# Order within a tile's period of block two's attention: scaling one tile ahead, high part in front of the next exponents, low part behind the next maxima

## The reference

```python
s_own = jnp.einsum("bhqd,bhkd->bhqk", qc, ko) * scale          # plus a bias by distance
p = jax.nn.softmax(logits, axis=-1)                            # attention over own tokens
...
s = jnp.einsum("bshd,bmhd->bhsm", q4, mk) * (MEM_DH ** -0.5)
p = jax.nn.softmax(s, axis=-1)                                 # attention over the memory
...
merged = sigmoid(ga + bg[0]) * y_a + sigmoid(gb + bg[1]) * y_b + sigmoid(gc + bg[2]) * y_c
x = x + rmsnorm(merged @ w_out, g_post_mix)
```

## Time and profile before

| what | value |
|---|---|
| median of 3 runs | 1616.34 us (1607.52 to 1617.88) |
| the profiled execution | 1616.58 us, span 1614.8 us |
| PE busy | 1515.2 us, 94% of the span |
| PEld, ACT, POOL, DVE busy | 1256.3, 656.9, 715.7, 583.3 us |
| self part of the attention, first transpose to last PV | 816.1 to 924.6 us |
| mem part | 1002.4 to about 1085 us |

### The profile page before, as it was taken

How to read it: one execution, slowest core, us unless ns; L and a number is a source line. 1 busy time by engine, 2 the same in 40 slices (tenths; PEclk the granted TensorE clock), 3 DMA queues, 4 the chain that set the end, 5 groups by cost and what they waited for, 6 DMA issues and landing times.

```text
span 1614.8 us, 19870 instructions
## 1 busy us (share of the span) xinstructions
PE 1515.2 (94%) x7716; PEld 1256.3 (78%) x7716; DVE 583.3 (36%) x888; ACT 656.9 (41%) x969; POOL 715.7 (44%) x608
## 2 busy tenths in 40 slices
PE   8899978899999999999987989999898999999996
PEld 5799757688888888888955678888787888887885
DVE  5755342523333110413034420433325556554002
ACT  3532453544444332322245443543335444554221
POOL 1466003545455544554412245445434455546452
PEclk9999888899999999999999999999999999999999
DMA  8654025322222222224111223122220222222221
GB/s 353 235 235 144 28 70 110 85 83 100 104 94 81 91 88 91 102 79 157 67 38 53 76 86 126 66 78 92 104 70 35 104 103 79 104 97 79 101 81 60
DMA packets 28491, 162.73 MB, mean 101 GB/s; under 512 B 4584, under 2 KB 4840, under 8 KB 13704
## 3 DMA queue, kind: packets, MB, share of 16 engines
q1 hardware_dynamic: 24960, 151.05, 26.0%
q10 hardware_dynamic: 3464, 10.74, 2.6%
HBM read 157.04 MB, written 4.74 MB: 100 GB/s over the span
## 4 chain that ended last, share of the span: by engine, by line
PE 68%; issue 11%; POOL 9%; DVE 5%; ACT 4%; DMA 3%; POOLq 0%; SPq 0%; ACTq 0%; DVEq 0%
PE ps L1695 60%; POOL WL L778 7%; PE ps L1661 1%; DMA raw<-w_up_dram 1%; DMA adap<-w_ada_dram 1%; POOL WL L742 1%; PE ps L1923 1%; DVE ps L1304 1%; ACT S L1110 1%; PE ps L1904 1%; PE ps L1828 1%; DVE S L1576 1%; PE ps L1617 1%; DVE xT L1309 1%; DVE md L1579 1%
## 5 line engine op out<-in xcount | busy, mean ns | idle before, releaser
L742 POOL TENSOR_TENSOR WL<-raw,WH 128x512 fp32r<-128x512 f32 (+2 forms) x344 | 370.4, 1105 | 541.1 <-ACT WH L858 540.9
L1695 PE MATMUL ps<-hH,WH 128*128 128x512 f32 x1136 | 455.5, 401 | 23.6 <-POOL hL L756 8.8
L1695 PE MATMUL ps<-hL,WH 128*128 128x512 f32 x1136 | 448.8, 395 | 0.0
L1695 PE MATMUL ps<-hH,WL 128*128 128x512 f32 x1136 | 448.0, 394 | 0.0
L778 POOL TENSOR_TENSOR WL<-raw,WH 128x512 fp32r<-128x512 f32 x176 | 246.6, 1432 | 240.4 <-ACT WH L1018 240.4
L1695 PEld LDWEIGHTS ps<-hH,WH 128*128 128x128 f32 x1136 | 216.9, 191 | 74.7 <-issue 26.3
L1695 PEld LDWEIGHTS ps<-hH,WL 128*128 128x128 f32 x1136 | 217.2, 191 | 46.3
L1695 PEld LDWEIGHTS ps<-hL,WH 128*128 128x128 f32 x1136 | 217.1, 191 | 43.8
L858 ACT ACTIVATE WH<-raw 128x1024 fp32r<-128x1024 f32 (+3 forms) x172 | 147.9, 885 | 235.8 <-PE ps L1695 228.2
L1695 PE MATMUL ps<-hidH,WH 128*128 128x512 f32 x352 | 137.9, 392 | 1.1 <-POOL WL L778 1.1
L1695 PE MATMUL ps<-hidL,WH 128*128 128x512 f32 x352 | 136.9, 389 | 0.0
(11 more groups left out here) (279 smaller groups left out, 2181.1 us busy)
## 6 DMA issues: line engine op xcount, KB each, us to landing
raw<-w_up_dram SPq DMA_DIRECT2D x44, 1024.0 KB, 4.8
raw<-w_in_dram SPq DMA_DIRECT2D x36, 1024.0 KB, 4.7
adaw<-w_ada_dram SPq DMA_DIRECT2D x22, 1024.0 KB, 6.5
raw<-w_down_dram SPq DMA_DIRECT2D x16, 768.0 KB, 3.9
raw<-w_down_dram SPq DMA_DIRECT2D x16, 640.0 KB, 3.7
xT<-x_dram ACTq DMA_DIRECT2D x2, 2048.0 KB, 10.0
raw<-w_mem_kv_dram SPq DMA_DIRECT2D x4, 1024.0 KB, 4.6
raw<-w_out_dram SPq DMA_DIRECT2D x4, 1024.0 KB, 4.5
```

The source lines that it names most:

```text
L742: pool.tensor_tensor(WL[:, d % 2, ks, cols], raw[:, d % 2, ks, cols], WH[:, d % 2, ks, cols].bitcast(F32), ALU.subtract).then_inc(lo_done, 1)
L1695: mm = pe.matmul(out, lhs[x], rhs[y], start=(first and i == 0), stop=(last and i == 2))
```

## The change

The handler of DVE's scaling is now a step of its own (`scale2`), which stands one tile ahead, in front of the next tile's maxima. ACT's high part is a step of its own (`hi2`), in front of the next exponents on ACT. The low part `lo2(n)` stands behind the maxima of tile n+2 on DVE and in front of the scaling of tile n+2. The new steps and `lo2` have no share of the pieces any more, so the pieces are dealt to `mid2`, `front2` and `back2` only, and stand at other places between PE's steps. Both the self and the mem part are ordered so. No instruction is added or removed, and the streams of POOL and SP are the same.

```diff
         def attend(first, last, pieces):
-            tiles = [("front2", first), ("front2", first + 1)]
+            tiles = [("front2", first), ("front2", first + 1), ("scale2", first)]
             for n in range(first, last):
                 tiles += [("mid2", n)]
-                if n > first:
-                    tiles += [("lo2", n - 1)]
+                if n + 1 < last:
+                    tiles += [("scale2", n + 1)]
+                tiles += [("hi2", n)]
                 if n + 2 < last:
                     tiles += [("front2", n + 2)]
-                tiles += [("back2", n)]
-            tiles += [("lo2", last - 1)]
-            share = [TILES23[tile[1]][3] + 1 for tile in tiles]
+                tiles += [("back2", n), ("lo2", n)]
+            share = [TILES23[tile[1]][3] + 1 if tile[0] in ("front2", "mid2", "back2") else 0 for tile in tiles]
...
-            def back2(n):
+            def hi2(n):
                 kind, i, c, _, _ = tile2(n)
                 sc.wait_ge(pv2_done, heads_before(n + 1))
...
-            def mid2(n):
+            def scale2(n):
                 kind, _, _, nb, heads = tile2(n)
                 ve.wait_ge(exp2_done, heads_before(n + 1))
```

More of the change, by code:

```diff
@@ L1153, in _ @@
                   "bias_fetch": bias_fetch, "bias_rows": bias_rows, "evac_in2": evac_in2, "bias_load": bias_load, "evac_br": evac_br,
-                  "front2": front2, "mid2": mid2, "back2": back2, "mem_load": mem_load,
+                  "front2": front2, "mid2": mid2, "hi2": hi2, "mem_load": mem_load,
                   "evac_kv": evac_kv, "merge": merge})
@@ L1607, in _ @@
                   "attn_out": attn_out, "up": up,
-                  "bias_rows": bias_rows, "evac_in2": evac_in2, "evac_br": evac_br, "front2": front2, "mid2": mid2,
+                  "bias_rows": bias_rows, "evac_in2": evac_in2, "evac_br": evac_br, "front2": front2, "scale2": scale2,
                   "lo2": lo2, "merge": merge})
```

## The result

The changed kernel takes 1600.44 us (median of 8, 1593.02 to 1606.60), the kernel before 1615.12 us (median of 8, 1607.52 to 1619.80). The ratio is 0.9914, with an interval of 0.9894 to 0.9934, so 10.7 to 17.1 us, 13.9 in the middle. The forecast was 7 us of gain and a range that ended at 1602: the direction was right, the size was half of what came.

The account below looks back on a forecast made before the run. PE bounds the kernel, so only its waits can be won: 14.9 us of old self-part waits against 7.5 new gives 7.4 gain, mem part none; 1616.58 - 7.4 = 1609.2, predicted 1609 us, own range 1606 to 1613, wider range 1602 to 1617.

Parts of the forecast that it names:

- Tiles 2, 4 and 5: Self part, transposes following a PV with no piece behind it: PE waits for the low part, 0.45 + 0.35 + 0.35 = 1.15 us.
- Gate 64: Sigmoid gate of unit 64 on ACT, self part near tile 6: its queue makes PE wait 1.4 us; before, 1.95.
- Gates 65 and 67: Gates of units 65 and 67 on DVE, self part, now in front of the low part: 0.7 us of wait each.
- Gate 68: Gate of unit 68 on ACT, tile 14: queue of exponents, split, gate, PT makes PE wait 3.5 us, the worst.
- Old ones: PE's standing time in the self part before the change, 14.9 us, all counted as going away.
- the bound of 16.4 us: Most the change could win: PE's standing time in self and mem parts, 14.9 + 1.5 us, 1.0% of 1616.6.
- both dips: Two stretches of PE at 1.2 GHz at the self part's start, both taken to stay; the second's going would gain about 1.6 us.
- up to 1.4 goes: Mem part: PE's waits for the scaling, up to 1.4 us, could go; none counted, as the first tile's chain holds part.
- the rival in which all waits are covered: Self part: ACT's queues slip less, only 2.5 us of new waits remain; gain 12.4 to 14, 1602.5 to 1604 us; chance 0.15.
- Waits moved to ACT: Slower rival: ACT's exponents, split, gate and PT queue starts late, 23 us of new waits against 14.9; 1625 us; chance 0.08.
- No gain at the end: Rival: time won in the part is given back behind it or by stretched scalings; 1615 to 1617 us; chance 0.15.
- The table rule: About 1380 ns drain per table switch: gates 64 and 68 each cost 1.38 us more, gain 4.6 instead of 7.4; not adopted.

Follow-up runs that it names:

- the last kernel: Changed kernel with the gates of units 64, 65, 67 and 68 moved behind transposes or low parts, and a piece after every self-part PV: 1593.28 us, ratio 0.9878.

## Why the prediction was wrong

**Right: each new wait.** The forecast had 7.5 us of new waits in the self part at named places; 7.1 came at the same places. Tiles 2, 4 and 5, with no piece behind the PV before, 0.56 + 0.45 + 0.45 for a forecast 1.15. Gate 64 at tile 6, 1.20 for 1.4. Gates 65 and 67 on DVE, at tiles 7 and 12, 0.44 and 0.54 for 0.7 each. Gate 68, 3.50 for 3.5. Gate 66 nothing. That the sum is so near is partly luck: 0.3 us too little at the tiles and 0.6 too much at gates 64, 65 and 67 go against each other. These readings came from laying two queues side by side, instruction by instruction, and the move of gate 68 shows that the queue is the cause. The scaling waits went to zero, but for the very first transposes'.

**Wrong: idle time as the price of a wait.** The step was "New waits: 1.15 + 1.4 + 1.4 + 3.5 = 7.5 us. Old ones: 14.9. Gain 7.4 us in the self part." PE's idle fell by 7.7 (14.9 to 7.2), but the stretch fell by 9.4, and again by 9.5 in the run with the self part alone. PE's busy time fell too, by 1.7 us (94.94 to 93.22 in the windows of the table), for the same instructions. The clock doesn't explain it, since it cost 0.9 us more than before; less the clock's cost (3.1 and 4.0), the busy time fell from 91.8 to 89.2, by 2.6. A reason that fits: the ends of matmuls are modelled. In the changed kernel eight transposes in a row are followed by the next matmul 0.79 us after their start (893.00 to 893.79), 0.10 for each, yet one alone is counted as 0.27 long (the middle value of L1923 in the rows above). At a wait the last matmul's counted end isn't overlapped by the next, so 0.17 us more than the idle is lost; from 19 waits before to 7 after, behind the first transposes, that makes 12 x 0.17 = 2.0 us. And a short wait doesn't show at all. These are the eight transposes of tile 13 before:

```profile
904.58 1.28 PE L1923 MATMUL ps<-ident_t,S 128*128 128x128 f32 x8
904.79 0.29 DVE L1598 TENSOR_TENSOR bufBL<-ps,bufBH 128x128 fp32r<-128x128 f32 x1 [0.76 <-ACT bufBH L1128]
...
905.62 0.48 PE L1695 MATMUL ps<-hH,WH 128*128 128x512 f32 x1
```

No idle is counted, but they take 1.04 us instead of 0.79, since the second four may start only behind the low part, which ended at 905.08. Tile 14 is the same (913.78 to 914.82), so 0.5 us are hidden in the two, and 2.0 + 0.5 is close to 2.6. The other kernels agree roughly: less the clock's cost, PE is busy 91.8 us in the three with 19 or 20 waits, 90.4 with the scaling ahead only (13 waits), 89.1 to 89.5 in the four with 7, and 88.9 in the last one (2). No run changed the waits and nothing else, so this account is argued, not shown. It also corrects the bound of 16.4 us: in the last kernel the self part alone is 17.6 us shorter, more than the 14.9 that PE stood there.

**The clock.** The forecast let both dips stay and priced a further one at 1.6 us without counting it. One more came, behind gate 68, in all three profiles of the new self order. By the estimate of the table the clock cost 0.9 us more there than before, which hides a part of the gain.

**Wrong: the mem part at nothing.** The step was "In the mem part up to 1.4 goes; I count none", for a reason that didn't hold: the wait for the queries lies in front of the first scores and not in the 1.4. It gave 3.1 us alone (2.5 against the kernel without a change) and 3.7 in the changed kernel. The window of the earlier trace rows also ended at 1085.00, and a wait of 0.9 us for PT ended at 1086.47, behind its edge. The idle of 2.3 us and four waits at 0.17 make 3.0; the 0.6 us on top in the changed kernel are within the 0.6 by which this stretch also differs without a change.

With the two measured sizes in the sum the gain is 9.4 + 3.1 = 12.5 us, where the two comparisons gave 13.9 and 12.1. The start was off as well: the sum began at 1616.58, and the median of the eight runs of the kernel before is 1615.12. From there it gives 1602.6 us, where 1600.4 was measured; the rest is within what the comparison can tell.

**Wrong: the range.** Its lower end, 1602, came from the rival in which all waits are covered. That rival did not come true, as gate 68 shows; the gain came near its size by the two steps above, and the 1.5 us of the start did the rest.

**Rivals.** "Waits moved to ACT" is true at one of the three gates on ACT that have tiles behind them, gate 68, and only there does PT stand behind both the split and the gate. "No gain at the end" fell: what each part lost reached the end. The table rule that I weighed comes out by the rows: the load ends at 896.52 and the sigmoid starts at 896.54, and taking load and sigmoids out of the queue, 2.69 us, took 2.73 us off the wait. The Trainium skill's ScalarE: Activation LUTs, What ACT_TABLE_LOAD costs, states about 1380 ns of drain behind each load, by which an estimate for that is 4.1 us; the trace does not agree with it.

## What to carry to other kernels

In a pipeline of in-order queues, look for a short instruction that is ready and stands behind long ones that are not, and put it in front; here 0.26 us in front of 1.2 us of exponents took 7.2 us of waits away over 16 tiles, and 3.1 us came back at one gate. Judge such moves together: the scaling ahead alone gave nothing in the self part, and its absence cost the whole gain. Split a difference between two stretches in idle time, clock and the rest before giving it to the order. When you sum waits, count how many there are and look past the edges of the window, and check each rare step (a weight split, a table load) that the new order puts in front of something that the bound engine waits for.

## What the runs showed of the hardware

The self part repeats to 0.1 us from run to run when the clock's dips fall alike (99.5, 99.4, 99.4 us in three runs), while the whole time of one kernel spreads over 10 us or more, and 8.3 us of the lead of the profiled execution were made in front of the changed code. PE's granted clock in the self part was anything from 0.93 to 0.98 on average across these orders. It is made of single stretches at the lower level, 1.2 GHz: in all three profiles of the new self order one lies directly behind the wait of 3.50 us (mean 0.52 or 0.53 in 3.40 us), and with that wait down to 0.77 us it is gone. The wait of 1.95 us at tile 6 of the kernel before had none behind it. Two waits of PE of some 0.25 us in the kernel before did not show as idle time, and each one that shows costs some 0.17 us more than is counted, by the estimate above.
